# Decoder layer on one core: paired small products, eight compressed-key transposes joined into two, half-size value steps, and a new written-out step order

## What is computed

```python
# RWKV-7: decays and rates from two 64-wide low-rank projections, gate from a third
w = -jax.nn.softplus(-(w0 + jnp.tanh(wd) @ w_up)) - 0.5
a = jax.nn.sigmoid(a0 + ad @ a_up)
g = jax.nn.sigmoid(gd) @ g_up
...
# attention over 15 compressed keys, 8 heads in 2 groups
k_cmp = rms_norm(compress(kc.reshape(B, S, G, Dh), pe_k, ck_w1, ck_w2), kc_g)
v_cmp = compress(vc.reshape(B, S, G, Dh), pe_v, cv_w1, cv_w2)
s = jnp.einsum('bghqd,bgcd->bghqc', qb, k_cmp).astype(jnp.float32) * scale - slopes * dc.astype(jnp.float32)
p_c = masked_softmax(s, dc >= 0)
o_c = jnp.einsum('bghqc,bgcd->bghqd', p_c.astype(v_cmp.dtype), v_cmp)
...
# cross-attention, 4 heads of 256
q = rms_norm((hn @ xq_w).reshape(B, S, X_HEADS, X_HEAD_DIM), xq_g)
k = rms_norm((memn @ xk_w).reshape(B, M, X_HEADS, X_HEAD_DIM), xk_g)
v = (memn @ xv_w).reshape(B, M, X_HEADS, X_HEAD_DIM)
o = jnp.einsum('bhsm,bmhd->bshd', pr.astype(v.dtype), v).reshape(B, S, D)
```

## Time and profile before

| | |
|---|---|
| median of 3 runs | 1292.21 us (1291.49 to 1293.8) |
| the profiled execution | 1294.45 us, its span 1292.7 us |
| PE busy | 1241.8 us (96%) |
| DVE, ACT, POOL busy | 360.0, 191.8, 54.9 us |
| read from HBM | 440.75 MB, 342 GB/s over the span |
| mean granted TensorE clock | 0.993 of full |

### The profile page before, as it was taken

The page is one execution under the profiler, slowest core; times in us unless marked ns, Lnnn a source line. Parts: engine busy times, 40 slices in busy tenths (PEclk is TensorE's granted clock), DMA queues, the critical chain, the costliest instruction groups (busy, mean ns, idle before and its releaser), DMA issues.

```text
span 1292.7 us, 19115 instructions
## 1 busy us (share of the span) xinstructions
PE 1241.8 (96%) x7750; PEld 634.2 (49%) x7750; DVE 360.0 (28%) x846; ACT 191.8 (15%) x436; POOL 54.9 (4%) x104
## 2 busy tenths in 40 slices
PE   9999899899999999999999999999999998989897
PEld 8888788688883433323233333434333232333332
DVE  4466653432226212212121221212212121212111
ACT  3332354412320000000000000000000000000001
POOL 6210001101010000000000000000000000000000
PEclk9999899899999999999999999999999999999999
DMA  7342411068179999999999999999999999999997
GB/s 266 126 152 103 164 36 66 3 275 375 59 316 371 428 426 427 428 430 429 427 427 427 426 395 421 427 428 428 428 429 428 428 429 428 429 427 428 430 427 295
DMA packets 36055, 442.61 MB, mean 342 GB/s; under 512 B 4000, under 2 KB 4128, under 8 KB 6304
## 3 DMA queue, kind: packets, MB, share of 16 engines
q1 hardware_dynamic: 35424, 440.76, 81.7%
q10 hardware_dynamic: 576, 1.05, 0.2%
HBM read 440.75 MB, written 1.05 MB: 342 GB/s over the span
## 4 chain that ended last, share of the span: by engine, by line
PE 65%; DMA 31%; DVE 2%; ACT 1%; issue 1%; POOL 0%; SPq 0%; DVEq 0%; ACTq 0%; POOLq 0%
DMA sb_ring<-in_mlp_w 31%; PE ps L965 22%; PE ps L992 9%; PE ps L323 9%; PE ps L923 3%; PE ps L933 2%; PE ps L677 2%; PE ps L821 2%; PE ps L772 2%; PE ps L543 2%; PE ps L945 1%; PE ps L336 1%; PE ps L980 1%; PE ps L418 1%; PE ps L401 1%
## 5 line engine op out<-in xcount | busy, mean ns | idle before, releaser
L965 PE MATMUL ps<-sb_ring,sb_xv 128*64 128x512 f32 x1960 | 439.7, 596 | 29.4 <-DMA sb_ring<-in_mlp_w 28.5
L965 PEld LDWEIGHTS ps<-sb_ring,sb_xv 128*64 128x64 f32 x1960 | 133.5, 137 | 311.5 <-issue 252.7
L992 PE MATMUL ps<-sb_ring,sb_xv 128*64 128x512 f32 x1024 | 228.5, 596 | 1.3 <-DMA sb_ring<-in_mlp_w 1.3
L1558 DVE TENSOR_SCALAR sb_early<-ps 128x256 f32<-128x256 f32 x64 | 27.2, 424 | 646.5 <-PE ps L965 646.5
L992 PEld LDWEIGHTS ps<-sb_ring,sb_xv 128*64 128x64 f32 x1024 | 71.7, 137 | 134.6 <-issue 132.8
L1598 ACT ACTIVATE sb_early<-sb_early 128x256 f32<-128x256 f32 (+2 forms) x69 | 28.2, 408 | 510.1 <-DVE sb_early L1558 507.3
L1598 ACT ACTIVATE sb_early<-ps 128x512 f32<-128x512 f32 (+4 forms) x46 | 23.6, 515 | 280.2 <-PE ps L992 265.9
L933 PE MATMUL ps<-sb_early 64*128 64x512 f32 x248 | 61.6, 615 | 0.0
L923 PE MATMUL ps<-sb_early,sb_hnT 128*128 128x128 f32 x512 | 59.9, 275 | 0.0
L923 PEld LDWEIGHTS ps<-sb_early,sb_hnT 128*128 128x128 f32 x512 | 58.4, 192 | 0.2 <-DVE sb_early L1439 0.2
L323 PE MATMUL ps<-sb_hnT,sb_wsl 128*128 128x256 f32 x256 | 56.1, 379 | 0.0
(11 more groups left out here) (359 smaller groups left out, 1068.3 us busy)
## 6 DMA issues: line engine op xcount, KB each, us to landing
sb_ring<-in_mlp_w SPq DMA_DIRECT2D x184, 2048.0 KB, 20.7
sb_wsl<-in_w_front SPq DMA_DIRECT2D x31, 1024.0 KB, 4.8
sb_ring<-in_mlp_w SPq DMA_DIRECT2D x4, 1024.0 KB, 17.9
sb_wsl<-in_mlp_w SPq DMA_DIRECT2D x3, 1024.0 KB, 7.6
sb_spare<-in_mlp_w SPq DMA_DIRECT2D x2, 1024.0 KB, 9.1
sb_wsl<-in_w_values SPq DMA_DIRECT2D x1, 1120.0 KB, 5.0
sb_wsl<-in_w_front ACTq DMA_DIRECT2D x4, 256.0 KB, 6.4
sb_ox<-in_mem_T SPq DMA_DIRECT2D x1, 1024.0 KB, 10.8
```

The lines of the kernel that those rows point to most:

```text
L965: mm = pe.matmul(psum[64 * half:64 * half + 64, 4 + n, :], xgT[:, k, SLOTS * par:SLOTS * par + SLOTS], w[:, at + 512 * half:at + 512 * hal ...
L992: mm = pe.matmul(psum[64 * o2:64 * o2 + 64, 7, :], actT[:, 2 * n + m, 64 * q:64 * q + 64], ring[:, at + 512 * o2:at + 512 * o2 + 512], sta ...
L1558: dve.tensor_scalar(gl, psum[:, 4 + n, 0:256], 7.0, None, ALU.min).then_inc(sem("glu"), 1)
```

## The change

- Decays and rates (`zw`, `az`): their products use rows 0 to 63 and rows 64 to 127 of the array, and are now issued in turn instead of one kind after the other.
- Keys' squares: POOL adds the two halves of `xsq` between ACT's square and `xnorm`, which then has one product instead of two.
- Compressed probabilities: a new step `turnc` transposes four heads of a group at once (`sc_c` padded to 32 columns a head), two transposes for 128 queries instead of eight; `h1T` and `vcmp` are laid out four times, so that `pv` picks its head by zeros. `vcmp` moves into `spare`, so the load (4, 1) moves behind (0, 1), at the front's end. POOL clears `h1T` and `vcmp` at the start.
- `xv` steps have 128 memory tokens each, eight instead of four.
- Cross `pv` takes a head's 256 queries at once: four steps instead of eight.
- `ORDER`, `CROSS` and the order of two weight loads are new.

The core of the diff (the lists by one line):

```diff
-LATE = [('xk_w', 0), ('xk_w', 1), ('xk_w', 2), ('xk_w', 3), ('cmp', 0), ('xv_w', 0), ('xv_w', 1), ('xv_w', 2),
+LATE = [('xk_w', 0), ('xk_w', 1), ('xk_w', 2), ('xk_w', 3), ('xv_w', 0), ('cmp', 0), ('xv_w', 1), ('xv_w', 2),
...
+        spare = sb("spare", 4096)
-        h1T = sb("h1T", NSA_G, NCMP)
+        h1T = sb("h1T", NSA_G, 4, 32)
...
-        vcmp, sc_c = view(early, 1536, 2, HD), view(early, 1664, TT, 8, 16)
-        ptc, xsq, xrs = view(early, 1920, 2, 2, P), view(early, 2816, 2, T), view(early, 3328, T)
+        vcmp, sc_c = view(spare, 2048, 4, 2, HD), view(early, 1664, TT, 8, 32)
+        ptc, xsq, xrs = view(early, 2176, TT, 2, P), view(early, 2816, 2, T), view(early, 3328, T)
-        xpt = view(hn, 1024, 2, 2, P)
+        xpt = view(hn, 1024, 2, 2, T)
...
-        ORDER = [('cmpin',), ('tok', 0), ('xk', 0), ('xk', 1), ('parts', 0), ('xkn', 0), ('xk', 2), ('xkn', 1),
+        ORDER = [('xk', 0), ('tok', 0), ('xkn', 0), ('cmpin',), ('parts', 0), ('xk', 1), ('tok', 3), ('xkn', 1),
...
-            for name, rows, w, act in (("zw", slice(0, 64), 0, wdad), ("az", slice(64, 128), 0, wdad),
-                                       ("gg", slice(0, 128), 1, gd)):
-                for i in range(2):
-                    t = tile(name, i, freed=(name, i + 1))
-                    for p in (2 * i, 2 * i + 1):
-                        mm = pe.matmul(t[:, (p % 2) * T:(p % 2 + 1) * T], lora[rows, w, p * P:(p + 1) * P],
-                                       act[rows, :], start=True, stop=True)
-                    mm.then_inc(sem("tile_ready"), 1)
+            for i in range(2):
+                decay, rate = tile("zw", i, freed=("zw", i + 1)), tile("az", i, freed=("az", i + 1))
+                for p in (2 * i, 2 * i + 1):
+                    for t, rows in ((decay, slice(0, 64)), (rate, slice(64, 128))):
+                        mm = pe.matmul(t[:, (p % 2) * T:(p % 2 + 1) * T], lora[rows, 0, p * P:(p + 1) * P],
+                                       wdad[rows, :], start=True, stop=True)
+                        if p % 2:
+                            mm.then_inc(sem("tile_ready"), 1)
+            for i in range(2):
+                t = tile("gg", i, freed=("gg", i + 1))
+                for p in (2 * i, 2 * i + 1):
+                    mm = pe.matmul(t[:, (p % 2) * T:(p % 2 + 1) * T], lora[:, 1, p * P:(p + 1) * P], gd,
+                                   start=True, stop=True)
+                mm.then_inc(sem("tile_ready"), 1)
...
-                    mm = pe.matmul(t[0:NCMP, g * HD:(g + 1) * HD], h1T[HD:P, g, :], cw2[HD:P, :],
-                                   start=True, stop=True)
+                    mm = pe.matmul(t[:, g * HD:(g + 1) * HD], h1T[HD:P, g, :, :].rearrange("p a b -> p (a b)"),
+                                   cw2[HD:P, :], start=True, stop=True)
...
-                pe.matmul(t[:, 0:T], o256[:, :], xsq[:, 0, :], start=True, stop=False)
-                pe.matmul(t[:, 0:T], o256[:, :], xsq[:, 1, :], start=False, stop=True) \
-                  .then_inc(sem("tile_ready"), 1)
...
-            def xv_step(j):
+                pe.matmul(t[:, 0:T], o256[:, :], xsq[:, 0, :], start=True, stop=True).then_inc(sem("tile_ready"), 1)
+            def xv_step(n):
+                j, tt = n // 2, n % 2
-                t = tile("xv", j, freed=("vx", j + 1))
-                rows_job(t, J_XV[j], lambda k, tt: memT[:, k, tt * P:(tt + 1) * P]) \
-                    .then_inc(sem("tile_ready"), 1)
+                t = tile("xv", n, freed=("vx", n + 1))
+                for k in range(KD):
+                    mm = pe.matmul(t[:, 0:T], memT[:, k, tt * P:(tt + 1) * P], wjob(J_XV[j])[:, k, :],
+                                   start=k == 0, stop=k == KD - 1)
+                mm.then_inc(sem("tile_ready"), 1)
...
+            def turnc_step(tt):
+                pe.wait_ge(sem("cmp_probs"), tt + 1)
+                t = tile("pc", tt, freed=("ptc", tt + 1))
+                for g in range(NSA_G):
+                    mm = pe.transpose(t[:, g * P:(g + 1) * P],
+                                      sc_c[:, tt, 4 * g:4 * g + 4, :].rearrange("p a b -> p (a b)"), ident[:, :])
+                mm.then_inc(sem("tile_ready"), 1)
-                if j == 0:
-                    pe.wait_ge(sem("cmp_probs"), tt + 1)
-                t = tile("pc", u, freed=("ptc", u + 1))
-                for g in range(NSA_G):
-                    mm = pe.transpose(t[0:NCMP, g * P:(g + 1) * P], sc_c[:, tt, 4 * g + j, 0:NCMP], ident[:, :])
-                mm.then_inc(sem("tile_ready"), 1)
...
-                pe.wait_ge(sem("ptc"), u + 1)
+                pe.wait_ge(sem("ptc"), tt + 1)
-                    pe.matmul(out_tile[0][64 * g:64 * g + 64, j * P:(j + 1) * P], vcmp[0:NCMP, g, :],
-                              ptc[0:NCMP, u % 2, g, :], start=True, stop=False)
+                    pe.matmul(out_tile[0][64 * g:64 * g + 64, j * P:(j + 1) * P], vcmp[:, j, g, :],
+                              ptc[:, tt, g, :], start=True, stop=False)
...
-            def xpv(n):
-                tt, i = n % 2, n // 2
-                pe.wait_ge(sem("xpt"), n + 1)
-                if n % 2 == 0:
-                    pe.wait_ge(sem("vx"), n // 2 + 1)
-                t = tile("xo", n, freed=("ox", n + 1))
+            def xpv(i):
+                pe.wait_ge(sem("xpt"), 2 * i + 2)
+                pe.wait_ge(sem("vx"), 2 * i + 2)
+                t = tile("xo", i, freed=("ox", i + 1))
-                        mm = pe.matmul(t[:, c * P:(c + 1) * P], vxm[:, m, i * X_HD + c * P:i * X_HD + (c + 1) * P],
-                                       xpt[:, n % 2, m, :], start=m == 0, stop=m == 1)
+                        mm = pe.matmul(t[:, c * T:(c + 1) * T], vxm[:, m, i * X_HD + c * P:i * X_HD + (c + 1) * P],
+                                       xpt[:, i % 2, m, :], start=m == 0, stop=m == 1)
...
-                link(dve.tensor_tensor(h1T[:, :, :], view(psum[:, b, 0:2 * NCMP], 0, NSA_G, NCMP),
-                                       view(csq, 0, NSA_G, NCMP), ALU.mult), "cmp_hidden")
+                link(dve.tensor_tensor(h1T[:, :, :, 0:NCMP],
+                                       bcast(view(psum[:, b, 0:2 * NCMP], 0, NSA_G, NCMP).unsqueeze(2), P, NSA_G, 4, NCMP),
+                                       bcast(view(csq, 0, NSA_G, NCMP).unsqueeze(2), P, NSA_G, 4, NCMP), ALU.mult),
+                     "cmp_hidden")
...
-                link(f(vcmp[0:NCMP, :, :], view(psum[0:NCMP, b, 0:P], 0, NSA_G, HD), ACT.Copy), "vcmp")
+                act.wait_ge(sem("vcmp_cleared"), 1)
+                for j in range(4):
+                    r = slice(32 * j, 32 * j + 32)
+                    link(f(vcmp[r, j, :, :], view(psum[r, b, 0:P], 0, NSA_G, HD), ACT.Copy),
+                         "vcmp" if j == 3 else "scalar_step")
...
+            def xv_step(n):
+                j, tt = n // 2, n % 2
+                b = ready(act, "xv", n)
+                link(f(vxm[:, tt, j * T:(j + 1) * T], psum[:, b, 0:T], ACT.Copy), "vx")
...
-                b = ready(act, "pc", u)
-                link(f(ptc[0:NCMP, u % 2, :, :], view(psum[0:NCMP, b, 0:2 * P], 0, 2, P), ACT.Copy), "ptc")
...
+            def turnc_step(tt):
+                b = ready(act, "pc", tt)
+                link(f(ptc[:, tt, :, :], view(psum[:, b, 0:2 * P], 0, 2, P), ACT.Copy), "ptc")
...
-                    if n >= 2:
-                        ready(act, "xo", n - 2)
-                    link(f(xpt[:, n % 2, :, :], view(psum[:, b, 0:256], 0, 2, P), ACT.Copy), "xpt")
+                    if i >= 2:
+                        ready(act, "xo", i - 2)
+                    link(f(xpt[:, i % 2, :, tt * P:(tt + 1) * P], view(psum[:, b, 0:256], 0, 2, P), ACT.Copy), "xpt")
...
-                    link(f(oxT[:, 2 * i:2 * i + 2, tt * P:(tt + 1) * P], view(psum[:, b, 0:256], 0, 2, P),
-                           ACT.Copy), "ox")
+                    link(f(oxT[:, 2 * n:2 * n + 2, :], view(psum[:, b, :], 0, 2, T), ACT.Copy), "ox")
...
+            link(pool.memset(h1T[:, :, :, :], 0.0))
+            link(pool.memset(vcmp[:, :, :, :], 0.0), "vcmp_cleared")
-                    ins = pool.tensor_scalar(sc_c[:, tt, i, :], distc[:, tt, :], 8.0 * SLOPE[i], None, ALU.mult)
+                    ins = pool.tensor_scalar(sc_c[:, tt, i, 0:NCMP], distc[:, tt, 0:NCMP], 8.0 * SLOPE[i], None,
+                                             ALU.mult)
...
+            def xk_step(j):
+                pool.wait_ge(sem("kx_squared"), j + 1)
+                pool.tensor_tensor(xsq[:, 0, :], xsq[:, 0, :], xsq[:, 1, :], ALU.add).then_inc(sem("kx_squares"), 1)
+                if step == "xk":
+                    xk_step(*args)
...
+                elif (n, half) == (4, 1):
+                    sp.wait_ge(sem("pv_done"), 8)
...
-                    piece_ahead(4, 1)
...
+            piece_ahead(4, 1)
```

59 lines of the change are left out of this document (24 added, 35 removed).

## The result

The changed kernel is slower: 1295.09 us median of 20 runs (1293.43 to 1302.49), against 1292.78 of 20 runs of the kernel before in the same measurement (1287.83 to 1296.71). The ratio is 1.0031, 95% interval 1.0017 to 1.0045, or +4.0 us (2.2 to 5.8); the two medians alone differ by 2.3. The profiled execution took 1295.15 us, its span is 1293.4 us.

The account below looks back on a forecast made before the run. PE ahead of the experts was taken as the bound. Terms -1.0 - 1.7 - 1.3 - 0.7 + 4.0 - 2.5 gave -3.2, with -0.3 added -3.5: from 1292.2 to 1288.7 us, range 1283 to 1293.5.

Parts of the forecast that it names:

- the clock term: PE's clock in the shared stage: two falls costing 5.5 us in place of before's 8.0, so -2.5 us.
- what I had added for waits that would disappear: Late in the shared stage: -0.3 us for waits that disappear because half `xv` steps stand there.
- The prediction's own alarm: Wrong if the front's end is over 6 us off 383.8 or the experts' length moves by over 1 us.
- Rival C: Chance 0.12: clock falls at three places, 5.0 us each, 15 instead of 5.5; slower, 1298, once loss is over 11.6.
- Less work in the small products: PE's work in the front: decays and rates -1.0 us, `xnorm` -1.7, compressed transposes -1.3.
- The gaps: PE's waits in the shared stage under the new order: 13.1 us against 9.1 before, so +4.0 us.
- Cross-attention, -0.7: Cross-attention: half as many `pv` records and fewer hand-overs to ACT, -0.7 us for the whole of it.
- Tables: ACT among the keys' steps: two more table loads at 1.28 us each, hidden behind PE's work, taken as 0.
- Rival D: Chance 0.07: the moved weight load holds up the experts, 1291.2 us.
- Rival E: Chance 0.06: POOL's four adds hold DVE ahead of `inv 0`, costing 2.9 us, 1291.6 us.
- Rival B: Chance 0.20: clock holds full through the long waits, or waits come out at half; -9.0 us, 1283 us.
- Rival F: Chance 0.10: the waits come out 3 us longer than worked out, so nothing is left, 1292 us.

Follow-up runs that it names:

- experiment 3: The changed kernel with idle products ahead of ten waits of PE, from the keys to cross-attention's first turns: 1289.43 us, 0.9989 of before.
- experiment 5: The changed kernel with idle products only at the stage's end waits (`turnp 6`, `chunk 0` to `chunk 2`): 1293.53 us, 1.0004 of before.
- experiment 6: The changed kernel with idle products only at the earlier waits (`xkn 0`, `xkn 1`, `cmpout`, `inv 10`): 1291.53 us, 1.0002 of before.
- experiment 11: The changed kernel with `xnorm`'s two products back and no addition on POOL: 1298.64 us, 1.0049 of before.
- experiment 7: The changed kernel with two half `xv` steps moved, to ahead of `inv 10` and ahead of `turnp 6`: 1288.83 us, 0.9966 of before.
- experiment 1: The changed kernel's smaller products in before's `ORDER`, `CROSS` and order of loads: 1292.44 us, 1.0011 of before.
- experiment 2: The changed kernel with the old `CROSS` alone, cross `pv` still merged: 1297.92 us, 1.0054 of before.
- experiment 9: experiment 7 with steps reordered to cover the early waits too, at `xkn 0`, `xkn 1` and `cmpout`: 1289.67 us, 0.9979 of before.
- experiment 4: The kernel before with idle products ahead of its longest waits (`cmpout`, `turnp 6`, chunks, first cross `turn`): 1293.78 us, 1.0013 of before.
- experiment 10: experiment 7 with idle products in its remaining waits: 1286.99 us, 0.9955 of before.
- experiment 8: experiment 1 with the new `CROSS`, `pv 6` ahead of `chunk 1` and `xv 6` between `chunk 1` and `chunk 2`: 1290.57 us, 0.9978 of before.

## Why the prediction was wrong

It said -3.5 and the chip says +4.0. At full clock it said -1.0 (the sum without the clock) and measured is +1.3. The clock it put at -2.5, and it is +2.7. So of the 7.5 us, 5.2 are the clock term and 2.3 the rest: 0.7 cross-attention, 0.3 the transposes, 0.5 the half `xv` steps, 0.3 what I had added for waits that would disappear, and 0.5 that lies within the fit's margin. PE's busy time before the experts fell by 3.4 us with the lost clock taken off (372.2 - 8.0 to 369.4 - 8.6), where 4 to 6 were forecast. The prediction's own alarm, a front's end more than 6 us off 383.8, stayed silent at 388.7: it was set too wide to catch an error of this size.

- *The clock term failed*, as the prediction put it: "I take two falls at the mean of a short one, 3.0, and a little less: 5.5 in place of 8.0". The 8.0 came from one execution of before; over its runs the loss is 6.3 to 7.3, on the mean 6.9. The changed kernel loses 10.5. Two places there are, as forecast, but each is worth about 5 on the mean and not 2.75 (experiments 3, 5 and 6), and the earlier of them lies behind `cmpout`, whose wait was to be shorter and was (1.4 for 1.9). The loss was also counted in full, and a lost microsecond costs 0.76. In the one profiled execution the loss is 6.9 + 1.7, near before's 8.0: a single profile would have hidden this term altogether. Rival C had the mechanism and the 5.0 for a fall, and asked for 11.6 in sum before it turned slower; with the other terms off, 10.5 was enough. Why each place costs more than in before isn't shown.
- *Less work in the small products was mis-sized*: -1.0 for decays and rates is right (4.72 to 3.76); its bound of -1.5 should read -1.4 (4.89 - 3.49). The keys' squares give 4 x 0.4 in work, but nothing in time (experiment 11). The transposes give 1.0 and not 1.3, since `turnc` takes 0.37 and not 0.22 (16 x 0.11 - 2 x 0.37). "Half `xv` steps cost the same columns as before" is true of columns and not of time: 8 x 3.56 = 28.5 against 4 x 7.0 = 28.0, by this row of before at 169.0 and the next at 176.0:

```profile
168.99 7.17 PE L677 MATMUL ps<-sb_wsl,sb_ox 128*128 128x256 f32 x32
176.00 0.38 PE L724 MATMUL ps<-sb_ident,sb_early 128*15 128x128 f32 x2
```

- *The gaps were right in sum*: 13.1 forecast, 13.1 measured. One by one: 1.4, 1.3 and 0.2 at `xkn` (1.25, 1.25, 0.2), 1.4 at `cmpout` (1.3), 2.1 at `inv 10` (3.0), 1.5 + 1.7 from `turnp 6` to `chunk 0` (4.1), 1.4 in the chunks (1.4). These make 11.0; the other 2.1, at `turnp 3`, `turnp 5`, `pv 4` and `yvar`, stand for a forecast of 0.6. So the two long chains came out 1.8 shorter than worked out and the small waits 1.5 longer, and that the sum fits to the tenth is luck. What I had under-read is what they mean: in experiment 7 3.9 of them went with two steps in another place.
- *Cross-attention, -0.7, failed.* It is 51.7 before and after at full clock. The term rested on half as many records and fewer hand-overs to ACT. Merged `pv` steps cost 2.3 us in the old order (experiments 1 and 2), and the new `CROSS` gives just that back.
- *Tables were right.* Both further loads are there, 1.28 us each, and `xkn 2` has no wait. The row at 131.37 ends and the next instruction follows 0.01 us later, in this timeline of ACT of the changed kernel; and in experiment 9 the load at 153.58 stands 0.01 us behind a copy. The Trainium skill, ScalarE: Activation LUTs, section What ACT_TABLE_LOAD costs, comes to 2.66 us for a switch, with a drain. These traces show 1.28 us, and no drain on either side of the two loads.

```profile
131.37 1.28 ACT L1596 ACT_TABLE_LOAD   x1 [4.81 <-DVE sb_st L1373]
132.66 0.40 ACT L1596 ACTIVATE sb_qx<-sb_qx,sb_st 128x128 f32<-128x128 f32 x1
...
137.29 1.28 ACT L1596 ACT_TABLE_LOAD   x1 [1.69 <-PE ps L672]
```

- *Rival D (the moved load) is out*, by the 4.77 us from gather to first product. *Rival E (POOL holds DVE) isn't seen*: `inv 0` starts at 144.05 without a wait. *Rival B* describes what the filled changed kernel does to the clock, at 1289 and not 1283. *Rival F*, nothing left at full clock, is near the 1.3 measured there, but the waits didn't grow: the work shrank less. The experts kept their length to 0.7 us, inside the forecast's 1.

Two things stay open. Which activity of PE brings the clock down isn't settled, since experiment 4 kept its low stretch with short waits. And where the unprofiled runs lose their clock isn't seen, though experiments 5 and 6 and the low stretches of the fourteen profiles point to the same places. The 1.3 us at full clock are argued from rows and from the fit, whose margin is 0.6. What the experiments do show is that the order of steps is worth more here than the saved products: two steps moved give 4.8 us at full clock (experiment 7), and the smaller products in the old order 0.6 (experiment 1).

## What to carry to other kernels

Before saving work on the bounding engine, look up what it does right after: a product saved ahead of a wait gained nothing (experiment 11), and a merged step can't begin before its last input is there (experiments 1 and 2). Large independent steps are worth most as cover, so put them in front of the waits with the longest chains on other engines, and walk those engines' queues too, since a step put in front there delays what was to be covered (experiment 9). When a difference is below 1%, take the mean granted clock of every run, compare at equal clock, and forecast the loss from many runs rather than from one profile.

## What the hardware showed that I had not expected

- Runs of one kernel in one measurement differ by up to 10 us (before, measured with experiments 9 to 11, 1288.1 at a mean clock of 0.998 to 1298.5 at 0.989), most of it along one line in the granted clock.
- Idle products of 0.22 us in the waits of PE made the changed kernel 5.7 us faster with no step moved (experiment 3), and did nothing for the clock of before (6.1 lost for 6.3, experiment 4).
- The clock was low behind the wait at `cmpout` (1.4 to 3.6 us) in eight of nine profiles, and in none of the five in which idle products had cut that wait to 0.5 us or less. Behind a wait of 1.7 to 1.9 us at `tok 3` it was low in experiments 1, 4 and 8, and full in before.
